# Two small groups of TensorE work moved by one half unit in the branch loop of a hybrid decoder trunk

## The chip, the cores and the metric

The kernel runs on one core of a Trainium2 chip. The metric is the device time of one execution in microseconds (us); the kernel before takes 1792.09 us, the median of three executions (1791.9 to 1792.15).

## The reference

Two layers (DEPTH = 2) over one sequence of 512 tokens and 2048 channels, all in float32. Each layer projects its modulated input to twelve groups of 512 channels and feeds four branches with them: a gated short convolution, attention over eight heads, a gated linear recurrence (RG-LRU) and an S5 state space model. The four results are concatenated, mapped by one output projection and normalised. Cut to what matters here:

```python
h = x * (1.0 + scale[:, None]) + shift[:, None]
proj = h @ w_in[l]                     # (512, 2048) @ (2048, 6144)
q, k, v, b_g = jnp.split(pb, 4, axis=-1)
y_b = dilated_attention(q, k, v, rel_bias) * silu(b_g)
# RG-LRU, on the causal convolution xc of c_x, 8 block-diagonal heads of 64
r  = sigmoid(einsum('bshi,hij->bshj', xh, wa) + ba)
ig = sigmoid(einsum('bshi,hij->bshj', xh, wx) + bx)
log_a = -8.0 * r * softplus(-lam)
h_t = exp(log_a) * h_{t-1} + sqrt(-expm1(2 * log_a)) * ig * xc
y_c = h * silu(c_g)
# S5: drive bu = B u, a complex diagonal scan, y = Re(C x) + D u, GELU, GLU
y = concat([y_a, y_b, y_c, y_d]) @ w_out[l]
x = layer_norm(ALPHA * x + (1.0 + gate[:, None]) * y, ln_g[l], ln_b[l])
```

## The kernel before

**Tiling.** In each layer a hardware loop of four steps (`CT`, the variable `ct`) takes 128 channels of each of the twelve groups. A group of a step is a *unit* (`UNITS`: d_u, c_x, q, k, v, c_g, d_g, a_c, a_x, b_g, a_g, a_b), and a unit has two *half units*, each over half of the 2048 input channels, so a step has 24 half units, numbered n = 0 to 23. Both layers together run 8 such steps. After the four steps of a layer come its output projection and the normalisation.

**A half unit.** Each float32 operand is split into a high and a low part. For half unit n, TensorE runs 16 matmuls of 128x512 with the high part of the weights (L970 and L971 in turn, tile `w_hi`), then waits for the low part of the weights (`lo_ready`) and runs 8 more (L977, tile `w_lo`). The two parts of the weights have two buffers each, used in turn (`NHL` = 2).

**Where the weights come from.** SyncE loads them to `raw` (three buffers). ScalarE then does `split_hi(n)`: one instruction copies `raw` to `w_hi` (L604) once TensorE has finished the high part of half unit n-2, and a second writes minus the rounded value from `raw` to `w_lo` (L607) once TensorE has finished all of half unit n-2:

```python
act.wait_ge(s.hi_used.sem, s.hi_used.at(n + 1 - NHL, step) + ahead * HALF)
act.activation(w_hi[:, n % NHL, :], raw[:, n % NRAW, :], ACT.Copy).then_inc(s.hi_done.sem, 1)
act.wait_ge(s.mm_done.sem, s.mm_done.at(n + 1 - NHL, step) + ahead * HALF)
act.activation(w_lo[:, n % NHL, :], raw[:, n % NRAW, :], ACT.Copy, scale=-1.0)
```

GpSimd then issues a DMA that adds `raw` onto `w_lo` (L556); only when it has landed may L977 of half unit n run.

**The order on TensorE.** The small matmuls of the branches stand between half units, in an order written out by hand: `put(n, part)` places a part behind half unit n, and parts with the same n run in the order in which they were put. The parts of this case: `s5_turn` (n = 3), `s5_drive(q)` (5, 7, 10, 14; 32-row matmuls, L860), `lru_gates` (6; two full 128-row matmuls into banks 5 and 6, L878), `scores(t)` (9, 10, 12, 13; 64-row matmuls, L890) and `v_turn` (11; four full transposes into bank 7, L927).

**The order on ScalarE.** It is written out separately and is in program order. In the loop over n the body is `split_hi(n)` and then the copies and functions placed at n. `lru()` stands at n = 8:

```python
if n == 8:
    lru()
if n == 9:
    copy("k", k_t)
```

`lru()` first waits for both results of `lru_gates` (banks 5 and 6), then (L663 to L673) runs two Tanh, an Exp, a Tanh and a Sqrt, with a table load before the first and before the Sqrt. What it writes is read by VectorE, which does the recurrence and, behind it, `score_max(0)` on the first scores. The turned values of bank 7 are read at n = 14 (L713), where ScalarE waits for `s.full[7]`.

Of the kernel before, what the change touches and what calls it, by code (L numbers as in the profile page):

```python
# [122 lines left out]
def trunk(nc, A, out):  # L123
# [5 lines left out]
    with ExitStack() as ctx:  # L129
# [653 lines left out]
        def _(pe):  # L783
# [38 lines left out]
            for l, s in enumerate(layers):  # L822
# [11 lines left out]
                with pe.Fori(0, CT) as ct:  # L834
# [109 lines left out]
                    def put(n, part, *args):  # L944
                        between[n].append(lambda: part(*args))

                    put(3, s5_turn)
                    put(6, lru_gates)
                    for q, at in enumerate((5, 7, 10, 14)):
                        put(at, s5_drive, q)  # L950
                    put(19, s5_outputs)
                    for t, at in enumerate((9, 10, 12, 13)):
                        put(at, scores, t)
                    put(11, v_turn)
                    for g, (at_turn, at_weigh) in enumerate(((16, 18), (18, 20), (20, 22))):
                        put(at_weigh, weigh, g)
                        put(at_turn, p_turn, g)
# [124 lines left out]
        def branch_loop(dve, l, s, line, own, tt, ts, stt, repeat):  # L1082

            ADD, SUB, MUL = ALU.add, ALU.subtract, ALU.mult
            pr = {name: at for name, (at, _) in ROWS.items()}
            with dve.Fori(0, CT) as ct:
                counted = [s.own, s.to_act, s.p_norm, s.x_rot, s.xc_done, s.bb_done, s.step_end,
# [523 lines left out]
```

## Time and profile before

| | before |
|---|---|
| median of 3 executions | 1792.09 us |
| the profiled execution, its own time | 1796.57 us |
| its span, first to last instruction | 1794.8 us |
| mean granted TensorE clock | 0.962 of full speed |
| TensorE busy (matmul) | 1666.7 us, 93% |
| VectorE busy | 1219.8 us, 68% |
| ScalarE busy | 774.2 us, 43% |
| GpSimd busy | 233.3 us, 13% |

The profile shows one execution, whose own time is 4.5 us above the median; a change worked out from it is set against that execution and then carried over to the median. Matmuls overlap in the trace: one takes 0.39 us from start to end, but the next begins about 0.23 us after it, so lengths are best read from one start to another. Starts are in us from the span's start.

### The profile page before, as it was taken

Reading aid. Unit: us, or ns where it says so; the run is one execution under the profiler, and the core shown is the slowest. Engines: PE = TensorE matmul, PEld = TensorE weight load, DVE = VectorE, ACT = ScalarE, POOL = GpSimd, SP = SyncE. Lnnn points to the kernel's source line nnn. Section 1 sums busy time; section 2 is a strip of 40 time slices with the busy share of each in tenths; the row PEclk is TensorE's granted clock in tenths of the full one; section 3 lists DMA queues with packets and bytes.
Section 4 is the critical chain, followed back from the end, with each engine's and each line's share of the span. In section 5 each row is a group of like instructions: output and inputs, shape, how many; then the busy total and the mean of one; then the engine's idle time right before and its main releaser. Section 6 shows DMA issues by size and latency. Waiting matters only on the chain.

```text
span 1794.8 us, 23025 instructions
## 1 busy us (share of the span) xinstructions
PE 1666.7 (93%) x7527; PEld 1294.2 (72%) x7527; DVE 1219.8 (68%) x2338; ACT 774.2 (43%) x1022; POOL 233.3 (13%) x281
## 2 busy tenths in 40 slices
PE   2339999999999999999998999999999999999995
PEld 1327778777777777768886777877877777776884
DVE  5884894796688479657862576488468558743758
ACT  2125554653544555421127554554555464532120
POOL 2132111111111111000005111111111111100000
PEclk9559999999999999999997999999999999999998
DMA  7999889989988988858736788978988888855322
GB/s 255 369 349 254 212 208 241 231 222 229 222 223 209 237 227 213 237 166 292 224 121 178 178 187 205 221 185 188 218 198 195 198 203 193 186 166 206 134 95 104
DMA packets 322942, 376.05 MB, mean 210 GB/s; under 512 B 27064, under 2 KB 224032, under 8 KB 319784
## 3 DMA queue, kind: packets, MB, share of 16 engines
q1 hardware_dynamic: 294632, 272.36, 47.2%
q0 software_dynamic: 28224, 102.77, 31.9%
q8 instruction: 26, 0.43, 0.1%
q14 instruction: 60, 0.49, 0.1%
HBM read 261.81 MB, written 10.51 MB: 152 GB/s over the span
## 4 chain that ended last, share of the span: by engine, by line
PE 84%; DVE 8%; DMA 4%; ACT 2%; SPq 1%; issue 1%; POOL 0%; DVEq 0%; ACTq 0%; POOLq 0%
PE bank L970 19%; PE bank L977 19%; PE bank L971 18%; PE bank L1014 18%; DMA w_lo<-raw 3%; DVE work L1337 3%; DVE ada_acc L1337 2%; PE bank L860 2%; PE bank L994 2%; PE bank L890 1%; DVE y_t L1337 1%; PE bank L916 1%; PE bank L904 1%; PE bank L868 1%; PE bank L878 1%
## 5 line engine op out<-in xcount | busy, mean ns | idle before, releaser
L970 PE MATMUL bank<-op_hi,w_hi 128*128 128x512 f32 x1536 | 617.6, 402 | 0.0
L971 PE MATMUL bank<-op_lo,w_hi 128*128 128x512 f32 x1536 | 602.4, 392 | 0.0
L977 PE MATMUL bank<-op_hi,w_lo 128*128 128x512 f32 x1536 | 382.7, 391 | 7.4 <-DMA w_lo<-raw 7.4
L604 ACT ACTIVATE w_hi<-raw 128x1024 fp32r<-128x1024 f32 x196 | 207.8, 1060 | 399.1 <-PE bank L971 248.5
L970 PEld LDWEIGHTS bank<-op_hi,w_hi 128*128 128x128 f32 x1536 | 290.3, 189 | 94.2 <-issue 34.3
L977 PEld LDWEIGHTS bank<-op_hi,w_lo 128*128 128x128 f32 x1536 | 288.1, 188 | 71.6 <-DMA w_lo<-raw 12.2
L971 PEld LDWEIGHTS bank<-op_lo,w_hi 128*128 128x128 f32 x1536 | 290.4, 189 | 59.9 <-issue 1.9
L556 POOL DMA_DIRECT2D w_lo<-raw x196 | 170.9, 872 | 1056.2 <-ACT w_lo L607 1037.1
L607 ACT ACTIVATE w_lo<-raw 128x1024 fp32r<-128x1024 f32 x196 | 206.9, 1055 | 92.8 <-PE bank L977 92.7
L1337 DVE SCALAR_TENSOR_TENSOR ada_acc<-ada_in,cond,ada_acc 128x512 f32<-128x512 f32 (+1 forms) x234 | 181.5, 776 | 66.8 <-DMA ada_in<-in_w_ada 46.9
L744 ACT ACTIVATE w_hi<-raw 128x1024 fp32r<-128x1024 f32 x56 | 59.5, 1062 | 233.2 <-PE bank L1014 215.6
L1014 PE MATMUL bank<-w_hi,op_hi 128*128 128x512 f32 x480 | 147.9, 393 | 2.1 <-ACT op_hi L760 2.1
L1014 PE MATMUL bank<-w_hi,op_lo 128*128 128x512 f32 x480 | 145.8, 389 | 0.0
L1329 DVE TENSOR_TENSOR w_lo<-raw,w_hi 128x1024 fp32r<-128x1024 f32 x56 | 68.6, 1225 | 95.8 <-PE bank L1014 91.0
L1329 DVE TENSOR_TENSOR work<-bank,rot 128x512 f32<-128x512 f32 x128 | 88.5, 692 | 50.6 <-PE bank L860 46.5
L1014 PE MATMUL bank<-w_lo,op_hi 128*128 128x512 f32 x480 | 121.5, 392 | 0.0
L1014 PEld LDWEIGHTS bank<-w_hi,op_hi 128*128 128x128 f32 x480 | 90.2, 188 | 22.1 <-issue 3.2
L1014 PEld LDWEIGHTS bank<-w_lo,op_hi 128*128 128x128 f32 x480 | 91.0, 190 | 19.1
L1014 PEld LDWEIGHTS bank<-w_hi,op_lo 128*128 128x128 f32 x480 | 90.1, 188 | 18.8
L1329 DVE TENSOR_TENSOR work<-work 128x512 f32<-128x512 f32 x136 | 94.2, 692 | 4.6
L565 POOL TENSOR_TENSOR op_lo<-work,op_hi 128x512 fp32r<-128x512 f32 x32 | 51.5, 1619 | 288.0 <-ACT work L621 287.3
L1329 DVE TENSOR_TENSOR work<-work,rot 128x512 f32<-128x512 f32 x112 | 77.5, 692 | 3.8
(226 smaller groups left out, 1568.5 us busy)
## 6 DMA issues: line engine op xcount, KB each, us to landing
w_lo<-raw POOLq DMA_DIRECT2D x196, 512.0 KB, 5.1
raw<-in_w_in SPq DMA_DIRECT2D x192, 512.0 KB, 4.4
ada_in<-in_w_ada SPq DMA_DIRECT2D x256, 256.0 KB, 4.4
raw<-in_w_out SPq DMA_DIRECT2D x64, 512.0 KB, 4.1
raw<-in_w_ada SPq DMA_DIRECT2D x27, 512.0 KB, 7.2
ada_in<-in_w_ada SPq DMA_DIRECT2D x18, 512.0 KB, 7.6
rot<-in_w_ada SPq DMA_DIRECT2D x10, 512.0 KB, 7.1
bias_t<-in_w_ada SPq DMA_DIRECT2D x9, 512.0 KB, 7.5
```

The lines of the kernel that those rows point to most:

```text
L556: pool.dma_start(w_lo[:, n % NHL, :], raw[:, n % NRAW, :], accum_op=ALU.add)\
L565: pool.tensor_tensor(op_lo[:, k, :], hf[:, k % 2, :], op_hi[:, k, :].bitcast(F32), ALU.subtract).then_inc(s.op_lo.sem, 1)
L604: act.activation(w_hi[:, n % NHL, :], raw[:, n % NRAW, :], ACT.Copy).then_inc(s.hi_done.sem, 1)
L607: act.activation(w_lo[:, n % NHL, :], raw[:, n % NRAW, :], ACT.Copy, scale=-1.0)\
L744: act.activation(out_hi[slot_of(n)], raw[:, n % NRAW, :], ACT.Copy).then_inc(s.hi_done.sem, 1)
L860: fill(2 + i, pe.matmul(bank[2 + i][:, :], s5_w[row:row + 32, i, :], u[row:row + 32, :], start=True, stop=True))
L970: pe.matmul(o, w_hi[:, n % NHL, w], op_hi[:, k, :], start=k == 0, stop=False)
L971: mm = pe.matmul(o, w_hi[:, n % NHL, w], op_lo[:, k, :], start=False, stop=False)
L977: mm = pe.matmul(o, w_lo[:, n % NHL, w], op_hi[:, k, :], start=False, stop=k == KT - 1)
L1014: mm = pe.matmul(bank[4 * (c % 2) + t][:, :], x[:, k, P * t:P * (t + 1)], w[slot_of(n)][:, S * j:S * (j + 1)], start=i == 0 and j == 0 and ...
L1329: return dve.tensor_tensor(o, a, b, op)
L1337: return dve.scalar_tensor_tensor(o, a, sc, b, op0, op1)
```

## The change

The diff moves two lines of the order on TensorE:

```diff
@@ -945,13 +945,13 @@
                     put(3, s5_turn)
-                    put(6, lru_gates)
+                    put(7, lru_gates)
                     for q, at in enumerate((5, 7, 10, 14)):
                         put(at, s5_drive, q)
                     put(19, s5_outputs)
                     for t, at in enumerate((9, 10, 12, 13)):
                         put(at, scores, t)
-                    put(11, v_turn)
+                    put(12, v_turn)
                     for g, (at_turn, at_weigh) in enumerate(((16, 18), (18, 20), (20, 22))):
                         put(at_weigh, weigh, g)
                         put(at_turn, p_turn, g)
```

`lru_gates` is put before the drives, so at half unit 7 it runs ahead of `s5_drive(1)`; `v_turn` is put behind the scores, so at half unit 12 it runs behind `scores(2)`. TensorE issues as many instructions as before, and the rows of VectorE, ScalarE, GpSimd and SyncE are the same in both kernels.

TensorE between the low part of half unit 6 and half unit 8, before (the 16 matmuls with `w_hi` of a half unit are left out; L878 is `lru_gates`, L860 the drive):

```order
L977 MATMUL bank<-op_hi,w_lo 128x512 x8
L874 ISA
L878 MATMUL bank<-work,lru_w 128x512
L836 ISA
L878 MATMUL bank<-work,lru_w 128x512
L964 REGISTER_ALU
...
L977 MATMUL bank<-op_hi,w_lo 128x512 x8
L836 REGISTER_ALU
L860 MATMUL bank<-work,s_w 128x512 x2
```

The same place in the changed kernel:

```order
L977 MATMUL bank<-op_hi,w_lo 128x512 x8
L964 REGISTER_ALU
...
L977 MATMUL bank<-op_hi,w_lo 128x512 x8
L874 ISA
L878 MATMUL bank<-work,lru_w 128x512
L836 ISA
L878 MATMUL bank<-work,lru_w 128x512
L836 REGISTER_ALU
L860 MATMUL bank<-work,s_w 128x512 x2
```

The two gate matmuls now come behind a whole further half unit, directly ahead of the second drive.

ScalarE behind `split_hi(8)`, the same in both kernels (L661 and L662 are the waits for banks 5 and 6; the L604 and L607 at the end are `split_hi(9)`, L633 the copy of k):

```order
L663 ACT_TABLE_LOAD
L663 ACTIVATE work<-bank,lru_c 128x512
...
L673 ACT_TABLE_LOAD
L673 ACTIVATE work<-work 128x512
L602 REGISTER_ALU
L603 REGISTER_ALU
L604 ACTIVATE w_hi<-raw 128x1024
L607 ACTIVATE w_lo<-raw 128x1024
L633 ACTIVATE work<-bank 128x512
```

Nothing moved here: the waits for the gates, the five functions and then `split_hi(9)` still follow each other.

TensorE around half units 11 and 12, a piece of the difference (L927 is `v_turn`, L890 `scores(2)`):

```order
+L977 MATMUL bank<-op_hi,w_lo 128x512 x8
+L836 REGISTER_ALU
+L890 MATMUL bank<-work 128x192 x4
 L927 MATMUL bank<-ident,work 128x128 x4
-L964 REGISTER_ALU
...
-L977 MATMUL bank<-op_hi,w_lo 128x512 x8
-L836 REGISTER_ALU
-L890 MATMUL bank<-work 128x192 x4
```

The four transposes now follow the third scores, one half unit later.

## Rows read from the trace of the kernel before

**Rows 1.** The page's first part, TensorE: busy time, share, instructions.
```profile
PE 1666.7 (93%) x7527; PEld 1294.2 (72%) x7527; DVE 1219.8 (68%) x2338; ACT 774.2 (43%) x1022; POOL 233.3 (13%) x281
```

**Rows 2.** Waits of TensorE: line waited for, us in total, times, longest.
```profile
PE bank L977 <- DMA w_lo<-raw: 7.4, 7, 3.1
```

**Rows 3.** Timeline, TensorE: start, us, line; low parts of half units 6 to 9.
```profile
177.36 1.98 PE L977 MATMUL bank<-op_hi,w_lo 128*128 128x512 f32 x8
179.17 1.88 PE L878 MATMUL bank<-work,lru_w 128*128 128x512 f32 x4
...
184.56 1.98 PE L977 MATMUL bank<-op_hi,w_lo 128*128 128x512 f32 x8
...
191.28 1.98 PE L977 MATMUL bank<-op_hi,w_lo 128*128 128x512 f32 x8
...
196.72 1.98 PE L977 MATMUL bank<-op_hi,w_lo 128*128 128x512 f32 x8
```

**Rows 4.** Timeline, ScalarE: `lru()`, then `split_hi(9)` and the copy of k.
```profile
181.17 1.28 ACT L663 ACT_TABLE_LOAD   x1 [0.74 <-PE bank L878]
...
186.99 1.04 ACT L604 ACTIVATE w_hi<-raw 128x1024 fp32r<-128x1024 f32 x1
187.93 1.05 ACT L607 ACTIVATE w_lo<-raw 128x1024 fp32r<-128x1024 f32 x1
188.89 0.58 ACT L633 ACTIVATE work<-bank 128x512 f32<-128x512 f32 x1
```

**Rows 5.** Timeline, GpSimd: issues of the accumulating DMAs at three places.
```profile
189.27 0.86 POOL L556 DMA_DIRECT2D w_lo<-raw  x1 [7.70 <-ACT w_lo L607]
...
235.90 0.86 POOL L556 DMA_DIRECT2D w_lo<-raw  x1 [8.88 <-ACT w_lo L607]
239.97 0.98 POOL L556 DMA_DIRECT2D w_lo<-raw  x1 [3.21 <-ACT w_lo L607]
...
980.27 0.86 POOL L556 DMA_DIRECT2D w_lo<-raw  x1 [2.19 <-ACT w_lo L607]
982.91 0.87 POOL L556 DMA_DIRECT2D w_lo<-raw  x1 [1.77 <-ACT w_lo L607]
```

**Rows 6.** DMA issues around 189.27 and 235.90: the last number is us to landing.
```profile
w_lo<-raw POOLq DMA_DIRECT2D x1, 512.0 KB, 5.0
...
w_lo<-raw POOLq DMA_DIRECT2D x1, 512.0 KB, 5.7
```

**Rows 7.** Timeline, TensorE: the longest wait for a low part, and after.
```profile
988.28 3.78 PE L977 MATMUL bank<-op_hi,w_lo 128*128 128x512 f32 x8 [3.14 <-DMA w_lo<-raw]
991.85 0.63 PE L970 MATMUL bank<-op_hi,w_hi 128*128 128x512 f32 x1
...
996.73 1.98 PE L977 MATMUL bank<-op_hi,w_lo 128*128 128x512 f32 x8
```

**Rows 8.** Busy times in a stretch; third from the end: granted clock.
```profile
988.00:989.00 1.00, 0.72 (x2) 0.63 (x3) 0.00 (x0) 0.00 (x0) 0.00 (x0) 0.50 0.75 148
```

**Rows 9.** Timeline, TensorE: start of layer 0's output projection.
```profile
750.55 2.90 PE L1014 MATMUL bank<-w_hi,op_hi 128*128 128x512 f32 x8 [0.60 <-ACT op_hi L760]
753.25 3.03 PE L1014 MATMUL bank<-w_lo,op_hi 128*128 128x512 f32 x8
756.12 1.98 PE L1014 MATMUL bank<-w_hi,op_lo 128*128 128x512 f32 x8
```

**Rows 10.** Timeline, TensorE: a shorter wait, half unit 4 of step 3.
```profile
623.97 2.11 PE L977 MATMUL bank<-op_hi,w_lo 128*128 128x512 f32 x8 [1.13 <-DMA w_lo<-raw]
```

**Rows 11.** Timeline, TensorE: low parts of half units 10, 11 and 12.
```profile
202.98 1.98 PE L977 MATMUL bank<-op_hi,w_lo 128*128 128x512 f32 x8
...
210.35 1.98 PE L977 MATMUL bank<-op_hi,w_lo 128*128 128x512 f32 x8
...
216.28 1.97 PE L977 MATMUL bank<-op_hi,w_lo 128*128 128x512 f32 x8
```

**Rows 12.** Timeline, VectorE: where it waits for the first scores.
```profile
199.45 0.06 DVE L1222 MEMSET spare<- 128x1 f32 x1 [1.74 <-PE bank L890]
```

## The prediction

> **What bounds the kernel now.** I read the page first: TensorE is busy 93% of the span and no other engine over 68% [rows 1]. The list of waits then says that inside the branch loop it hardly waits: for the low part of the weights, 7.4 us in 7 waits over both layers [rows 2]. So the loop is paced by TensorE, and what must be asked of a change to its order is what it does to TensorE's own sequence, and whether the weights still come in time. For the first question the distance from one low part (L977) to the next serves as a ruler, since nothing overlaps in it. With nothing between two half units it is 196.72 - 191.28 = 5.44 us, of which 16 matmuls with the high part take 3.63 and 8 with the low part 1.81. Across `lru_gates` it is 184.56 - 177.36 = 7.20, so the gates cost 1.76 us; across `s5_drive(1)` it is 6.72, a cost of 1.28 [rows 3]. For the second question I read ScalarE and GpSimd behind the gates, where the way to the weights of half unit 9 runs through `lru()`.
>
> **The change part by part.** No instruction is added or removed, and no DMA is issued in another order.
>
> *The two joins.* A part behind another part no longer stands alone between two half units. The profile has one such pair already: behind half unit 10, a drive and `scores(1)` together cost 210.35 - 202.98 - 5.44 = 1.93 us [rows 11]. Alone the drive costs 1.28 and the smaller `scores(0)` 202.98 - 196.72 - 5.44 = 0.82 [rows 3, 11]. So that join saves at least 0.17 us, perhaps 0.3 since `scores(1)` is longer. But there both parts use a part of the array's rows, while the gates and the transposes use all 128, as the projection does. The row for the turn is small: 216.28 - 210.35 - 5.44 = 0.49 us for four transposes, each with its own weights [rows 11], which leaves little that stands for a boundary. So a join with these parts saves between nothing and 0.3 us; I take 0.1 for the turn. For the gates I take nothing, because their saving lies ahead of the wait below and is swallowed by it.
>
> The Trainium skill has a rule for this place: TensorEngine Tiling (Array Packing), under Key Properties, says that going from one tiling mode to another drains the array, while another tile of the same mode does not. By that rule neither join saves a drain, since the gates and the turn are in the projection's own mode: the two joins would bring 0 and not 16 x 0.17 = 2.7 us. No row here shows a drain by itself.
>
> *The gates one half unit later: ScalarE.* This is the term that decides. `lru_gates` starts at 179.17, as half unit 6 ends. In the changed kernel half unit 7 runs first, in 5.44 us, so the gates start at 184.61. ScalarE's first instruction for them comes 181.17 - 179.17 = 2.00 us after their start, when the second has ended, and it had then been idle for 0.74 us [rows 3, 4]: it already waits there. In the changed kernel it waits from about 180.4 to 186.61, with `split_hi(9)` queued behind it. `lru()` occupies it for 186.99 - 181.17 = 5.82 us, so the copy of the high part of half unit 9 starts at 192.43 in place of 186.99, the write of the negated part at 193.37, and GpSimd's issue, 1.34 us after that start now, at 194.71 in place of 189.27 [rows 4, 5]. All of it moves by 5.44 us.
>
> *What is late next.* The high part is ready at about 193.5, and half unit 8 ends at 191.28 + 1.81 = 193.1 [rows 3]. That is a first stall of 0.4 us. The DMA now lands 5.0 us after its issue [rows 6], at 194.27, and TensorE asks for it at 196.72: the margin is 2.45 us. Moved by 5.44 it is late by 5.44 - 2.45 = 2.99 us, which takes in the first stall.
>
> *How long the DMA takes then.* It will have company. `split_hi(10)` follows the copy of k at once, since half unit 8 is long done: 0.96 for the negation, about 0.52 for the copy of k and 0.94 for the next copy, so the next accumulating DMA is issued 2.4 us behind this one [rows 4]. The nearest row where one follows 4.07 us behind shows 5.7 us to landing; where one followed 2.64 us behind, and loads of `raw` too, PE went on 988.28 - 980.27 = 8.0 us after the issue [rows 5 to 7]. The bounds are 5.0 and 8.0. I take 5.4, between the two rows without that load beside them: the wait grows to 3.4 us. TensorE's first matmuls after a wait add 2.11 - 1.98 = 0.13 [rows 3, 10].
>
> *The clock.* After a wait of 1.13 us TensorE ran on as before [rows 10]. After the one of 3.14 us it ran at half the clock (granted clock 0.50, that is the 1.2 GHz level) [rows 8]: the low part took 991.85 - 988.28 = 3.57 in place of 1.94, and the next high part 996.73 - 991.85 = 4.88 in place of 3.63 [rows 7], a loss of 2.9 us. In another place a wait of 0.60 us behind sixteen one-column matmuls was followed by two groups of 2.70 and 2.87 us in place of 1.81 each, a loss of 1.95 [rows 9]. The new wait, some 3 us of nothing behind 3.6 us of full work, is nearest to the first. Per step the loss is 0 if the clock holds, 1.95 to 2.9 if it falls; I take the mean, 2.4.
>
> *The turn one half unit later* hides: its reader stands at n = 14 behind the negated part of half unit 14, which itself waits for half unit 12 and takes 1.05 us. `scores(2)` and the turn together take, by the rows above, somewhat over 0.82 + 0.49 us, so ScalarE waits a fraction of a us for the turn, and its next copy is held by half unit 13 anyway, which is still to run. *VectorE* gets the gates 5.44 us later, too. It needs them just before it waits 1.74 us for the first scores, and those move by the stall as well [rows 12]: nothing. SyncE's loads wait for the low parts of earlier half units and shift with TensorE.
>
> *Sum.* A step costs 3.4 + 0.13 - 0.1 = 3.4 us for the wait and 2.4 for the clock, 5.8 in all. The same order runs in all 8 steps, so 8 x 5.8 = 46.7 us (unrounded terms). The profiled execution, 1796.57, becomes 1843.3; carried to the median, 1792.09 becomes **1838.8**.
>
> **The rivals.**
> - *The clock holds.* The wait may be too short, or fall so that the activity around it keeps the clock. Half of the evidence for a fall is one wait of 3.14 us, and 1.13 us did nothing. Then 8 x 3.4 = 27 us remain: 1819. With a landing of 5.0 and both joins at 0.3, it is 8 x (2.99 + 0.13 - 0.3) = 22.6: 1815.
> - *The two DMAs hinder each other as at 980.27.* The landing is 8.0, the wait 6.0, the clock loss 2.9: 8 x 9.0 = 72, hence 1864. For it: the same spacing, 2.4 against 2.64. Against it: there a load of `raw` started in the same us, and here the next load waits until the stalled low part starts.
> - *Not slower: the joins win.* If ScalarE's late start costs TensorE nothing, there are two joins in each of 8 steps. At 0.3 us each they bring 4.8 us: 1787.3; at nothing, 1792. It decides where the gates' shift stays under the margin of 2.45 us, so it needs a `split_hi(9)` that does not pass through `lru()`, or a much shorter half unit. The order of ScalarE's rows is against it.
> - *That the change does not do what it says* is excluded by the rows of TensorE's order.
>
> **How the numbers follow.** The forecast has 0.60, with a range of its own of 1831 to 1846 (landing 5.0 with 1.95 for the clock; landing 5.7 with 2.9). The clock that holds has 0.24, the landing of 8.0 has 0.10, and the side that is not slower 0.06, split evenly between a gain and no change. The range from 1814 to 1856 takes in the first two; it ends at a landing of 7.0 with the full clock loss (8 x 8.0 = 64). A measurement of this kernel tells about 0.2% (3.6 us) from no change. So: faster 0.03, the same 0.03, slower 0.94.
>
> **What would show it.** Right: a wait of 2.5 to 3.5 us of L977 for the DMA of `w_lo` at half unit 9, 8 times, so some 25 us more under that releaser; a shorter one of L970 for ScalarE before it; ScalarE's wait for L878 up from 0.74 to some 6 us per step; stretches at half clock behind each wait, and a mean granted clock below 0.962. The clock step is wrong if the clock stays at full speed in those places. The whole is wrong if half unit 9 starts its low part without a wait, or if ScalarE's table load comes 2.00 us behind the gates and its copy for half unit 9 does not follow it. The joins: in the distances between low parts, the sum over half units 11 and 12 should be 0.1 us less than now.

## The result and the profile after

The changed kernel takes 1822.06 us, the median of 4 executions (1820.06 to 1828.17), against 1792.12 us before: a ratio of 1.0169 with a 95% interval of 1.0143 to 1.0195, some 30 us slower. The profiled execution has a span of 1818.2 us and a mean granted clock of 0.960.

The waits of TensorE (line waited for, us in total, times, longest), to hold against [rows 2]:

```profile
PE bank L977 <- DMA w_lo<-raw: 20.1, 13, 2.5
...
PE bank L970 <- ACT w_hi L604: 2.1, 8, 0.3
```

Both new waits are there, the second in all 8 steps. The timeline of TensorE in step 0, low parts of half units 6 to 9 with the gates and the drive, to hold against [rows 3] (start, us, line; in brackets the idle time before and what ended it):

```profile
177.53 1.98 PE L977 MATMUL bank<-op_hi,w_lo 128*128 128x512 f32 x8
182.97 1.97 PE L977 MATMUL bank<-op_hi,w_lo 128*128 128x512 f32 x8
184.79 1.88 PE L878 MATMUL bank<-work,lru_w 128*128 128x512 f32 x4
186.59 1.13 PE L860 MATMUL bank<-work,s_w 32*128 32x512 f32 x4
191.45 1.97 PE L977 MATMUL bank<-op_hi,w_lo 128*128 128x512 f32 x8
193.70 0.50 PE L970 MATMUL bank<-op_hi,w_hi 128*128 128x512 f32 x1 [0.28 <-ACT w_hi L604]
...
199.54 2.10 PE L977 MATMUL bank<-op_hi,w_lo 128*128 128x512 f32 x8 [1.92 <-DMA w_lo<-raw]
...
205.93 1.97 PE L977 MATMUL bank<-op_hi,w_lo 128*128 128x512 f32 x8
```

Half unit 7 is now clean (182.97 - 177.53 = 5.44), and from 7 to 8 it is 8.48: the 1.76 us of the gates went from one distance to the other, to the hundredth. From half unit 8 to 9 it is 199.54 - 191.45 = 8.09 in place of 5.44: 2.65 us late. The rows in brackets show only 0.28 and 1.92 us of it. Such a row begins when the last matmul has ended, 0.16 us after the next one could have begun (0.39 - 0.23), so each of the two waits costs 0.16 more than its row. The 0.13 us that are left are the slower start of the high part behind the first wait (its first matmul takes 0.50 in place of 0.39): 0.28 + 0.16 + 1.92 + 0.16 + 0.13 = 2.65. ScalarE and GpSimd show why, to hold against [rows 4, 5]:

```profile
186.79 1.28 ACT L663 ACT_TABLE_LOAD   x1 [6.18 <-PE bank L878]
...
192.60 1.04 ACT L604 ACTIVATE w_hi<-raw 128x1024 fp32r<-128x1024 f32 x1
193.55 1.04 ACT L607 ACTIVATE w_lo<-raw 128x1024 fp32r<-128x1024 f32 x1
194.50 0.58 ACT L633 ACTIVATE work<-bank 128x512 f32<-128x512 f32 x1
194.98 1.05 ACT L604 ACTIVATE w_hi<-raw 128x1024 fp32r<-128x1024 f32 x1
```

```profile
194.89 0.86 POOL L556 DMA_DIRECT2D w_lo<-raw  x1 [13.13 <-ACT w_lo L607]
197.27 0.86 POOL L556 DMA_DIRECT2D w_lo<-raw  x1 [1.52 <-ACT w_lo L607]
```

The DMA issues at these two times (the last number is us to landing), to hold against [rows 6]:

```profile
w_lo<-raw POOLq DMA_DIRECT2D x1, 512.0 KB, 4.6
...
w_lo<-raw POOLq DMA_DIRECT2D x1, 512.0 KB, 5.4
```

ScalarE stands idle for 6.18 us (0.74 before) with the split of half unit 9 behind it, and the issue comes 5.45 us later than before, relative to half unit 6. The DMA lands in 4.6 us, sooner than the 5.0 of before. VectorE's wait for the first scores grew from 1.74 us to 4.50:

```profile
202.41 0.06 DVE L1222 MEMSET spare<- 128x1 f32 x1 [4.50 <-PE bank L890]
```

It waits for more, not for less: it is not what holds TensorE. The clock, in step 1 (timeline of TensorE, then stretches with the granted clock third from the end):

```profile
346.51 1.97 PE L977 MATMUL bank<-op_hi,w_lo 128*128 128x512 f32 x8
348.75 0.50 PE L970 MATMUL bank<-op_hi,w_hi 128*128 128x512 f32 x1 [0.27 <-ACT w_hi L604]
354.57 2.82 PE L977 MATMUL bank<-op_hi,w_lo 128*128 128x512 f32 x8 [1.89 <-DMA w_lo<-raw]
364.09 1.08 PE L977 MATMUL bank<-op_hi,w_lo 128*128 128x512 f32 x4
```

```profile
354.00:355.00 1.00, 0.43 (x2) 0.39 (x3) 0.00 (x0) 0.00 (x0) 0.00 (x0) 1.00 1.04 197
356.00:357.00 1.00, 1.00 (x4) 0.57 (x2) 0.00 (x0) 0.00 (x0) 0.00 (x0) 0.50 1.11 131
359.00:360.00 1.00, 1.00 (x4) 0.81 (x3) 0.85 (x4) 0.00 (x0) 0.63 (x1) 0.50 0.14 28
361.00:362.00 1.00, 1.00 (x4) 0.71 (x3) 0.97 (x2) 0.00 (x0) 0.00 (x0) 0.50 1.04 197
```

From half unit 9 to 10 it is 364.09 - 354.57 = 9.52 us. Step 0 takes 205.93 - 199.54 = 6.39 for the same, behind an equal wait (1.92 against 1.89), and in the kernel before it was 6.26 [rows 3, 11]. So the clock fell to its lower level (1.2 GHz) in one step and not in the other. In the 8 steps of this execution it fell in three, for 3.1, 3.1 and 1.6 us.

**The sum.** Over the 8 steps, from the distances between low parts: half unit 9 late, 8 x 2.67 = 21.4 us; half unit 9 to 10 slower than the 6.26 of before without a fall of the clock, 8 x 0.15 = 1.2; the clock, 7.8; the joined turn, 8 x -0.08, some -0.7. That is 29.7 us, and the medians differ by 29.9. The two profiled spans differ by only 23.4 us, because the profiled execution of before had its 3.14 us wait and the fall of the clock behind it [rows 7]; the one after waited 2.54 us there and the clock held, 3.5 us less in that place. A further 1.6 us less lies between the two layers' loops, the rest mostly in shorter waits at half unit 4 of other steps.

### The profile page after: what moved, and what is told of

It is laid out like the page before. It is cut to its first block, busy times and chain, and to the rows that moved or that the text cites. A ratio compares the mean times of both kernels' runs of the same rounds, so it can differ in the third digit from the quotient of the medians.

```text
span 1818.2 us, 23025 instructions
## 1 busy us (share of the span) xinstructions
PE 1674.7 (92%) x7527; PEld 1294.5 (71%) x7527; DVE 1221.2 (67%) x2338; ACT 773.3 (43%) x1022; POOL 232.7 (13%) x281
## 4 chain that ended last, share of the span: by engine, by line
PE 79%; DVE 7%; DMA 6%; ACT 4%; issue 2%; SPq 1%; POOL 0%; ACTq 0%; DVEq 0%; POOLq 0%
PE bank L977 18%; PE bank L1014 18%; PE bank L970 17%; PE bank L971 17%; DMA w_lo<-raw 4%; DVE work L1337 2%; DVE ada_acc L1337 2%; PE bank L994 2%; PE bank L890 1%; PE bank L860 1%; DVE y_t L1337 1%; PE bank L916 1%; PE bank L904 1%; DMA raw<-in_w_ada 1%; PE bank L868 1%
## 5 line engine op out<-in xcount | busy, mean ns | idle before, releaser
L977 PE MATMUL bank<-op_hi,w_lo 128*128 128x512 f32 x1536 | 385.6, 393 | 20.2 <-DMA w_lo<-raw 20.1
L604 ACT ACTIVATE w_hi<-raw 128x1024 fp32r<-128x1024 f32 x196 | 207.7, 1060 | 365.7 <-PE bank L971 220.9
L977 PEld LDWEIGHTS bank<-op_hi,w_lo 128*128 128x128 f32 x1536 | 288.0, 189 | 88.2 <-DMA w_lo<-raw 28.9
L556 POOL DMA_DIRECT2D w_lo<-raw x196 | 171.1, 873 | 1081.4 <-ACT w_lo L607 1061.9
L607 ACT ACTIVATE w_lo<-raw 128x1024 fp32r<-128x1024 f32 x196 | 206.8, 1055 | 105.6 <-PE bank L977 105.3
L1014 PEld LDWEIGHTS bank<-w_hi,op_hi 128*128 128x128 f32 x480 | 89.9, 188 | 22.1 <-issue 3.2
L1014 PEld LDWEIGHTS bank<-w_hi,op_lo 128*128 128x128 f32 x480 | 90.1, 188 | 18.7
```

The costliest lines, as they stand in the source:

```text
L556: pool.dma_start(w_lo[:, n % NHL, :], raw[:, n % NRAW, :], accum_op=ALU.add)\
L977: mm = pe.matmul(o, w_lo[:, n % NHL, w], op_hi[:, k, :], start=False, stop=k == KT - 1)
L1014: mm = pe.matmul(bank[4 * (c % 2) + t][:, :], x[:, k, P * t:P * (t + 1)], w[slot_of(n)][:, S * j:S * (j + 1)], start=i == 0 and j == 0 and ...
```

## The experiments

The theory after the result: ScalarE works its queue in order, so its wait for the gates holds back the split of half unit 9; the weights' DMA then comes late. The rivals: TensorE's own order or the turn costs the time; VectorE gets the gates too late; the DMA queues are what is late, whatever ScalarE does.

**The gates alone.**

```diff
-                    put(6, lru_gates)
+                    put(7, lru_gates)
```

> The gates at half unit 7, the turn left at 11. Theory (ScalarE's queue: its wait for the gates holds back the split of half unit 9): the whole slowdown stays, 2.65 us per step at the low part of half unit 9 plus half clock behind some of these waits, so 1820 to 1826 us, and the 0.08 us per step that the joined turn gave are missing. Rival (the move of the turn costs, for instance through ScalarE's wait for bank 7): this kernel is clearly faster than the changed one, below 1810.

Measured: 1821.93 us, ratio 1.0164 (1.0145 to 1.0183). The low part of half unit 9 is 2.55 to 3.01 us late in the 8 steps. The slowdown is all here.

**The turn alone.**

```diff
-                    put(11, v_turn)
+                    put(12, v_turn)
```

> The turn at half unit 12, the gates left at 6. Theory: 8 x 0.08 = 0.6 us less than before, about 1791.5, within what the measurement can tell. Rival (the turn has a share in the slowdown): above 1796.

Measured: ratio 0.9987 (0.9974 to 1.0000), median 1791.18. From half unit 11 to 12 TensorE takes 5.44 in place of 5.94 (in six of the eight steps), from 12 to 13 it takes 6.93 in place of 6.51: 0.08 us less per step; in the other two it is 0.09. The turn has no share in the slowdown.

**ScalarE's order changed instead of TensorE's.**

```diff
-                        if n == 8:
-                            lru()
                         if n == 9:
+                            lru()
                             copy("k", k_t)
```

> The changed kernel with ScalarE's work on the gates placed behind the split of half unit 9 and ahead of the copy of k, TensorE's order as changed. Theory: the wait at half unit 9 is gone, and the time is that of before less the joined turn: 1791 to 1793. Rival (the cost lies in TensorE's own order: gates joined with a drive, or in the recurrence that comes later on VectorE): the time stays at 1815 or more.

Measured: 1792.46 us, ratio 0.9997 (0.9986 to 1.0008): the 30 us are gone, with the gates on TensorE where the change put them. ScalarE and then TensorE in this run's timeline (the kernel has one line less, so L977 is L976 here):

```profile
182.38 1.06 ACT L604 ACTIVATE w_hi<-raw 128x1024 fp32r<-128x1024 f32 x1 [2.56 <-PE bank L970]
184.19 1.06 ACT L607 ACTIVATE w_lo<-raw 128x1024 fp32r<-128x1024 f32 x1 [0.75 <-PE bank L976]
185.99 1.28 ACT L663 ACT_TABLE_LOAD   x1 [0.74 <-PE bank L877]
```

```profile
190.66 1.98 PE L976 MATMUL bank<-op_hi,w_lo 128*128 128x512 f32 x8
196.10 1.98 PE L976 MATMUL bank<-op_hi,w_lo 128*128 128x512 f32 x8
```

The split of half unit 9 now comes ahead of the table load, and from half unit 8 to 9 it is 5.44 again. VectorE gets the gates at the late time in this kernel, too, and nothing comes of it. Both rivals, the order of TensorE and the late gates on VectorE, fall.

**A shorter way through ScalarE.** The Sqrt and its table load are left out:

```diff
-                        act.activation(lru_s[0], lru_s[0], ACT.Sqrt).then_inc(s.from_act.sem, 1)
+                        act.sem_inc(s.from_act.sem, 1)
```

> The changed kernel without the Sqrt of the recurrent branch and the table load ahead of it (the square root of the multiplier is left out, so the recurrence is fed with another number). ScalarE's work behind the gates is shorter by 1.28 + 0.54 = 1.82 us. Theory: the low part of half unit 9 comes 2.65 - 1.82 = 0.83 us late in place of 2.65, the trace's wait there falls from 1.9 to about 0.1 to 0.8 us, and the clock falls behind none: 8 x 0.83 less 0.6 = 6 us over before, 1798. A table load may turn up elsewhere. Rival (the wait comes from the DMA queue, whatever ScalarE does): the time stays above 1812.

Measured: 1820.94 us, ratio 1.0147 (1.0113 to 1.0182). This was a clear miss (1798 forecast). The issue did come 1.6 us sooner, but the low part is 2.64 to 2.94 us late in layer 0, no less than in the changed kernel, and 1.86 to 2.39 in layer 1. GpSimd's issue in step 1, then the DMAs issued around it:

```profile
350.73 0.86 POOL L556 DMA_DIRECT2D w_lo<-raw  x1 [11.56 <-ACT w_lo L607]
```

```profile
w_lo<-raw POOLq DMA_DIRECT2D x1, 512.0 KB, 6.3
ada_in<-in_w_ada SPq DMA_DIRECT2D x1, 256.0 KB, 4.2
```

It lands 6.3 us after its issue, in place of 4.6 in the changed kernel. So the rival on the DMAs has a part: ScalarE's delay alone doesn't set the wait. SyncE issues the load of `raw` for half unit 11 and then the loads of `ada_in` right behind the start of the low part of half unit 8, and this DMA now meets them while they run.

**A longer way in the changed kernel.** Two more copies into a tile that is overwritten:

```diff
+                        for i in range(2):
+                            if i:
+                                act.wait_ge(s.act_own.sem, s.act_own.at(i, ct))
+                            act.activation(lru_s[2], bank[6][:, :], ACT.Copy).then_inc(s.act_own.sem, 1)
```

> The changed kernel with two more copies of a 128x512 tile on ScalarE ahead of its work on the gates (their result is overwritten), about 1.3 us per step. Theory: the low part of half unit 9 comes 2.65 + 1.3 = 3.95 us late, 8 x 1.3 = 10 us more, and with waits of some 3.2 us in the trace the clock falls behind most of the 8, not behind three: 5 x 2.9 = 14 us more. Together about 1846. Rival (the fall of the clock doesn't go with the length of the wait): about 1832.

Measured: 1833.92 us, ratio 1.0223 (1.0192 to 1.0254). The low part is 3.71 to 3.77 us late, 1.1 more than in the changed kernel, so the wait grew by what ScalarE lost; here the DMA lands in 4.5 to 4.6 us. The additional wait stands ahead of the high part (1.43 us in step 0, 0.28 in the changed kernel), and the wait for the DMA is no longer than in the changed kernel (1.79 to 1.88 us). The clock fell in 4 of 8 steps, not in most, so the forecast of 1846 missed, and the time is near the rival's 1832.

**A longer way in the kernel before, within the margin.** The same two copies.

> The kernel before with the same two copies, about 1.3 us per step. Theory: the margin of 2.45 us hides them: 1792, with no wait at half unit 9. Rival (the margin was read wrongly, so that every microsecond on ScalarE counts): 1802.

Measured: ratio 1.0001 (0.9985 to 1.0018), no wait at half unit 9. The DMA is issued 1.17 us later and lands in 5.7 us in step 1; that is still 0.6 us ahead of the time at which TensorE asks for it.

**Beyond the margin.** Five copies.

> The kernel before with five such copies, about 3.3 us per step. Theory: 3.3 - 2.45 = 0.85 us late per step, 7 to 8 us in all, with no fall of the clock: 1799 to 1800. If the margin is 2.45 us, the wait at half unit 9 shows it to a tenth. Rival (VectorE or the scores become late instead): waits elsewhere.

Measured: 1830.38 us, ratio 1.0209 (1.0176 to 1.0243), about five times the slowdown that was expected. The issue moved by 3.07 us, but the low part is 2.3 to 3.7 us late. Step 1: GpSimd's issue, the DMAs issued around it, and TensorE (L977 is L982 here):

```profile
351.67 0.86 POOL L556 DMA_DIRECT2D w_lo<-raw  x1 [10.75 <-ACT w_lo L607]
```

```profile
w_lo<-raw POOLq DMA_DIRECT2D x1, 512.0 KB, 8.0
ada_in<-in_w_ada SPq DMA_DIRECT2D x1, 256.0 KB, 4.8
```

```profile
350.62 1.98 PE L982 MATMUL bank<-op_hi,w_lo 128*128 128x512 f32 x8
359.68 2.11 PE L982 MATMUL bank<-op_hi,w_lo 128*128 128x512 f32 x8 [3.46 <-DMA w_lo<-raw]
366.12 1.98 PE L982 MATMUL bank<-op_hi,w_lo 128*128 128x512 f32 x8
```

The landing takes 8.0 us in this place. Behind this wait of 3.46 us, the longest but one at half unit 9 in these runs, the clock did not fall: 366.12 - 359.68 = 6.44.

**Which neighbour holds the DMA back.** Two runs, both without the Sqrt. The first moves the loads of `ada_in` away:

```diff
-ADA_AT = (1, 2, 4, 5, 7, 8, 10, 11, 13,
+ADA_AT = (1, 2, 4, 5, 7, 8, 10, 12, 13,
```

> The changed kernel without the Sqrt (as the run without it), and with the two loads for the next conditioning (one in layer 1) that SyncE issues at half unit 11 moved to 12, so that they don't run beside the weights' DMA for half unit 9. Theory 1 (those loads hold that DMA back): its landing falls from 6.3 us to about 5, and the low part of half unit 9 is 1.5 us late in place of 2.8 in layer 0. Theory 2 (the next accumulating DMA, 2.4 us behind, holds it back): no change at half unit 9.

Measured: 1805.2 us in its one execution. Step 1: the DMA issued at 348.18, then TensorE:

```profile
w_lo<-raw POOLq DMA_DIRECT2D x1, 512.0 KB, 4.8
```

```profile
346.32 1.98 PE L977 MATMUL bank<-op_hi,w_lo 128*128 128x512 f32 x8
353.00 2.11 PE L977 MATMUL bank<-op_hi,w_lo 128*128 128x512 f32 x8 [1.08 <-DMA w_lo<-raw]
```

The DMA lands in 4.8 us in place of 6.3, the low part is 1.24 to 1.46 us late over the 8 steps, and the clock falls in none. With that, ScalarE's time counts again: against the changed kernel the issue comes 1.56 us sooner, the landing takes 0.2 us longer, and the low part comes 1.38 us sooner in step 1. The second run keeps those loads and moves the next accumulating DMA away:

```diff
                             copy("k", k_t)
+                            for i in range(5):
+                                act.wait_ge(s.pad_own.sem, s.pad_own.at(i, ct))
+                                act.activation(pad[:, :], ident[:, :], ACT.Copy).then_inc(s.pad_own.sem, 1)
```

> The changed kernel without the Sqrt, and with five small copies (128x128, about 0.4 us each) on ScalarE between the copy of k and the split of half unit 10, so that the accumulating DMA for half unit 10 is issued about 4.4 us behind that for 9 in place of 2.4. Theory 2 (the next accumulating DMA holds it back): landing 5.0 to 5.5 us for half unit 9 in place of 6.3. Theory 1 (the loads do): 6.3 as before.

Measured: 1824.4 us in its one execution. GpSimd's two issues in step 1 (L556 is L558 here), then the first one's landing:

```profile
353.45 0.86 POOL L558 DMA_DIRECT2D w_lo<-raw  x1 [11.56 <-ACT w_lo L609]
357.39 0.86 POOL L558 DMA_DIRECT2D w_lo<-raw  x1 [3.09 <-ACT w_lo L609]
```

```profile
w_lo<-raw POOLq DMA_DIRECT2D x1, 512.0 KB, 6.4
```

The next one comes 3.94 us behind in place of 2.37, and the first still lands in 6.4 us. So in the kernel without the Sqrt it is the loads of `ada_in` that hold the DMA back, not the accumulating DMA behind it. With five copies more those loads were not moved; that they make the 8.0 us there is inferred from this case.

Put together for step 1, in us from the low part of half unit 6 (the load of `raw` is issued at 14.3, the first of `ada_in` at 14.8, the second at 15.7 in the kernel before, 16.3 with two copies more and 15.4 in the others that have it):

| kernel | issue | landing after | landed at |
|---|---|---|---|
| before | 11.9 | 5.0 | 16.9 |
| before, two copies more | 13.1 | 5.7 | 18.7 |
| before, five copies more | 15.0 | 8.0 | 22.9 |
| changed, no Sqrt | 15.8 | 6.3 | 22.1 |
| the same, `ada_in` loads moved | 15.8 | 4.8 | 20.6 |
| changed | 17.4 | 4.6 | 21.9 |
| changed, two copies more | 18.5 | 4.6 | 23.1 |

An issue at 15.0 lands later than one at 17.4. Between the two, in step 1, ScalarE gains TensorE nothing by being sooner while those loads stay in place.

**Joins between parts that both use part of the array's rows.** The second drive goes to the first scores:

```diff
-                    for q, at in enumerate((5, 7, 10, 14)):
+                    for q, at in enumerate((5, 9, 10, 14)):
```

> The kernel before with the second drive moved from half unit 7 to 9, where it stands ahead of the first scores: both use a part of the array's rows. Theory (a join pays only between parts that both use less than all rows, as behind half unit 10): 0.17 to 0.3 us per step, 1.4 to 2.4 us in all, 1789.7 to 1790.7. Rival 1 (any join saves about 0.1): 1791.3. Rival 2 (VectorE gets the drive too late): slower than before.

Measured: ratio 0.9985 (0.9975 to 0.9994), median 1790.47 against 1793.53 for the kernel before beside it. From half unit 7 to 8 it is 1.28 us less, from 9 to 10 it is 1.06 us more: 0.22 saved in each of the 8 steps, 1.8 us in all. That is within the ratio's interval (1.1 to 4.5 us less), and the first rival's 0.1 per step falls by the distances.

**A version that beats both.**

```diff
-                    for q, at in enumerate((5, 7, 10, 14)):
+                    for q, at in enumerate((5, 9, 10)):
...
-                    put(11, v_turn)
+                    put(13, s5_drive, 3)
+                    put(12, v_turn)
```

> The kernel before with the turn behind the third scores (half unit 12), the second drive ahead of the first scores (9) and the fourth drive behind the fourth scores (13, was 14). Theory: the turn brings 0.08 us per step and each join of a drive with scores 0.22, as the second drive did at 9: 8 x 0.52 = 4.2 us less than before, about 1788 to 1789 against 1792 to 1793. Rival (at 13 the fourth drive has to wait for VectorE to free banks 2 and 3): TensorE waits there and the gain of that join is gone, 1790 or more.

Measured: ratio 0.9972 (0.9961 to 0.9982), median 1791.09 against 1796.03 for the kernel before beside it, 5 us less, where 4.2 were forecast. Step 1, low parts of half units 12 to 15 (L977 is L978):

```profile
367.51 1.97 PE L978 MATMUL bank<-op_hi,w_lo 128*128 128x512 f32 x8
374.44 1.98 PE L978 MATMUL bank<-op_hi,w_lo 128*128 128x512 f32 x8
382.23 1.98 PE L978 MATMUL bank<-op_hi,w_lo 128*128 128x512 f32 x8
387.67 1.98 PE L978 MATMUL bank<-op_hi,w_lo 128*128 128x512 f32 x8
```

The distance behind the fourth scores is 7.79 with the drive in it, and the next is a clean 5.44. Before they were 6.73 and 6.72: 0.22 us saved, and no wait for VectorE at the drive. So the rival falls. The gain is that of the three joins: 8 x (0.08 + 0.22 + 0.22) = 4.2 us.

## Why the prediction was right, and where its sizes were off

**Right: the mechanism, its place and each link.** The forecast was that ScalarE waits at the gates with the split of half unit 9 queued behind it. Its idle time went from 0.74 to 6.18 us (some 6 forecast), the issue from 189.27 to 194.89 (194.71 forecast; all of half unit 6 is 0.17 later in this execution), with a first short wait for the high part and the longer one for the low part in all 8 steps. The sign "a wait of 2.5 to 3.5 us of L977" was not met as a row: the 8 rows are 1.81 to 2.45 us, since the landing was shorter and a part of the lateness lies ahead of the high part. The run with ScalarE's order changed settles it: with that alone the cost is gone. The 1822.06 us lie within the range of 1814 to 1856, but the likeliest case's 1838.8 is 17 us too high, outside its own range of 1831 to 1846, and near the rival in which the clock holds (1819). The range held because it took in that rival too, and not because the likeliest case was right.

**Off: the landing.** The step "I take 5.4, between the two rows without that load beside them" should have been 4.6 in layer 0 and 4.5 to 5.1 in layer 1. The wait was 2.67 us on average, not 3.4: 8 x 0.7 = 6 us of the error. The reasoning that the next accumulating DMA 2.4 us behind would slow this one was wrong: it followed 2.38 us behind, and this one landed in 4.6 us; the run with the larger gap shows no effect of it in the kernel without the Sqrt either. In the changed kernel no load of `raw` runs beside this DMA's second half, since the next such load waits for the stalled low part, and the loads of `ada_in` were issued 2.6 and 2.0 us ahead of it. That this is why it lands sooner than before was not tried by itself.

**Off: the clock.** "I take the mean, 2.4" stood for a fall in every step. It fell in three of eight, 7.8 us in place of 19: 11 us of the error. That a wait of nearly the observed length is nearest to the row with the fall was the wrong reading: in the runs an equal wait was followed by a fall in one step and not in the next. The size of one fall, 1.6 or 3.1 us, lay outside the bounds of 1.95 to 2.9 on either side; the mean of the three, 2.6, lay within them.

**Right: the joins and the rule beside them.** The gates' join brought nothing: 1.76 us left one distance and came to the next. The turn's brought 0.08 us (0.1 forecast). Two joins of parts that both use part of the rows brought 0.22 each. By the rule on tiling modes in TensorEngine Tiling (Array Packing), Key Properties, of the Trainium skill, the gates' join saves nothing, and the trace agrees; for the turn it says 0 too, and what its 0.08 us are stays open.

**Not in the prediction, found by the runs: the margin of 2.45 us is not a number of ScalarE's alone.** It took the landing of 5.0 us as fixed while the issue moves. Here the cost rose from nothing (issue at 13.1) to 2.3 to 3.7 us per step (15.0), and at the changed kernel's 17.4 it was no higher (2.6 to 3.2). The forecast for five copies failed by this (1799 forecast, 1830 measured), and the one without the Sqrt as well (1798 and 1821).

## What to carry to other kernels

Where a consumer works its queue in order, moving its producer by one slot moves all that stands behind the consumer's wait; look at what is queued there, and move the consumer's place with the producer's. A margin at a DMA holds only as long as the DMA keeps its neighbours: ask which transfers are issued at the new time, since 3 us of delay took its landing from 5.0 to 8.0 us here. And on TensorE, put small parts together that use only a part of the array's rows (32 and 64 here); joining them with full ones brought next to nothing here.

## What the runs showed of the hardware

Between 1.7 and 3.6 us, the fall of the granted clock to 0.50 behind a wait did not clearly go with the wait's length. Over the six kernels with waits of 1.7 to 3.6 us at half unit 9 it fell behind 18 of 48: 13 of 36 waits under 2.6 us and 5 of 12 above. Four of the 13 are in the kernel with two copies more, which has a further wait of some 1.4 us ahead of the high part. It did not fall behind one wait of 3.46 us, and it fell behind one of 1.78 us. Behind the 8 waits of 1.08 to 1.30 us it never fell. One fall cost 1.5 to 1.7 or some 3.1 us, once 4.3. What decides between a fall and none in this range stays open. The accumulating DMA of 512 KB, 4.5 us at its fastest, took 8.0 us when it was issued 0.6 us behind a load of `raw` and 0.2 us behind one of `ada_in`, with a second load of `ada_in` 0.4 us behind it; the first load of `ada_in` landed in 4.8 us.
